# Delta inverse in 32-row corners, and the scaling of the delta rows on VectorE

## What is computed

```python
kb = kc * bc[..., None]
A = jnp.where(strict, einsum("bhncd,bhnsd->bhncs", kb, kc) * decay, 0.0)
rhs = jnp.concatenate([vc * bc[..., None], kb * jnp.exp(gc)[..., None]], axis=-1)
sol = lax.linalg.triangular_solve(A, rhs, left_side=True, lower=True, unit_diagonal=True)
u, w = sol[..., :Dv], sol[..., Dv:]
kdec = kc * jnp.exp(gc[..., -1:] - gc)[..., None]

def step(state, inp):
    v_new = u_i - einsum("bhcd,bhde->bhce", w_i, state)
    o = einsum("bhcd,bhde->bhce", qg_i, state) + einsum("bhcs,bhse->bhce", aqk_i, v_new)
    state = state * gl_i[..., None, None] + einsum("bhcd,bhce->bhde", kdec_i, v_new)
    return state, o
```

## Time and profile before

| | |
|---|---|
| median of three runs | 2746.93 us (2744.68 to 2751.48) |
| the profiled execution | 2750.94 us |
| its span | 2749.2 us, mean granted clock 0.995 |
| TensorE matmul | 2705.3 us busy (98%) |
| TensorE weight load | 2372.3 us (86%) |
| VectorE | 2091.8 us (76%) |
| ScalarE | 1265.3 us (46%) |
| GpSimd | 56.9 us (2%) |
| the delta inverse, first product to `w` | 130.71 to 176.93 us in the first layer |

### The profile page before, as it was taken

How to read it: one execution, slowest core, us unless ns; L and a number is a source line. 1 busy time by engine, 2 the same in 40 slices (tenths; PEclk the granted TensorE clock), 3 DMA queues, 4 the chain that set the end, 5 groups by cost and what they waited for, 6 DMA issues and landing times.

```text
span 2749.2 us, 52010 instructions
## 1 busy us (share of the span) xinstructions
PE 2705.3 (98%) x20739; PEld 2372.3 (86%) x20748; DVE 2091.8 (76%) x3771; ACT 1265.3 (46%) x1926; POOL 56.9 (2%) x89
## 2 busy tenths in 40 slices
PE   9999999999999999999999999999999999999998
PEld 7887898886998689998999998886999999999886
DVE  6766887766775569999666667885999976666787
ACT  4534554433553444455444445442555444444543
POOL 0010000020000000000000000000000000000000
PEclk9999999999999999999999999999999999999999
DMA  5305884314883135643555557663564355555764
GB/s 212 108 34 230 320 325 151 110 41 190 329 329 140 68 129 191 231 150 114 187 193 185 184 192 259 241 232 129 188 230 166 116 177 191 183 185 193 248 243 170
DMA packets 95348, 515.07 MB, mean 187 GB/s; under 512 B 18384, under 2 KB 24912, under 8 KB 38352
## 3 DMA queue, kind: packets, MB, share of 16 engines
q1 hardware_dynamic: 74256, 485.11, 48.9%
q10 hardware_dynamic: 20928, 27.63, 2.9%
HBM read 494.88 MB, written 17.83 MB: 186 GB/s over the span
## 4 chain that ended last, share of the span: by engine, by line
PE 81%; DVE 16%; issue 1%; ACT 1%; DMA 0%; POOL 0%; DVEq 0%; ACTq 0%; SPq 0%; POOLq 0%
PE bank L917 19%; PE bank L905 19%; PE bank L944 12%; PE bank L2089 8%; DVE ring_r L2671 3%; PE bank L2345 3%; PE bank L730 3%; PE bank L581 2%; PE bank L789 2%; PE bank L2363 1%; DVE sb L2754 1%; DVE sb L2745 1%; PE bank L659 1%; DVE sb L2746 1%; PE bank L560 1%
## 5 line engine op out<-in xcount | busy, mean ns | idle before, releaser
L2089 PE MATMUL bank<-peer_pass_high,q_high 128*128 128x256 f32 x1232 | 356.4, 289 | 1.3 <-DVE ring_r L2705 0.8
L2089 PE MATMUL bank<-h_low,q_high 128*128 128x256 f32 x1232 | 347.7, 282 | 0.0
L2089 PE MATMUL bank<-peer_pass_high,ring_r 128*128 128x256 f32 x1232 | 347.1, 282 | 0.0
L917 PE MATMUL bank<-peer_pass_high,peer_pass_hidden 128*128 128x512 f32 x1024 | 339.5, 393 | 0.0
L905 PE MATMUL bank<-peer_pass_high 128*128 128x256 f32 x1008 | 283.2, 281 | 0.0
L905 PE MATMUL bank<-peer_pass_high,ring_r 128*128 128x256 f32 x1008 | 282.9, 281 | 0.0
L905 PE MATMUL bank<-hT_r,peer_pass_high 128*128 128x256 f32 x1008 | 282.9, 281 | 0.0
L1023 DVE TENSOR_TENSOR ring_r<-ring,peer_pass_high 128x1024 fp32r<-128x1024 f32 x128 | 156.8, 1225 | 155.2 <-ACT peer_pass_high L1663 155.2
L2089 PEld LDWEIGHTS bank<-peer_pass_high,q_high 128*128 128x128 f32 x1232 | 233.8, 190 | 1.9 <-DVE ring_r L2705 1.0
L2089 PEld LDWEIGHTS bank<-peer_pass_high,ring_r 128*128 128x128 f32 x1232 | 233.4, 189 | 0.0
L2089 PEld LDWEIGHTS bank<-h_low,q_high 128*128 128x128 f32 x1232 | 232.7, 189 | 0.0
(11 more groups left out here) (431 smaller groups left out, 6324.0 us busy)
## 6 DMA issues: line engine op xcount, KB each, us to landing
ring<-in_experts SPq DMA_DIRECT2D x256, 1024.0 KB, 4.8
ring<-in_w SPq DMA_DIRECT2D x137, 1024.0 KB, 4.8
sb<-in_w_mod SPq DMA_DIRECT2D x48, 1024.0 KB, 6.7
sb<-spill SPq DMA_DIRECT2D x64, 256.0 KB, 5.0
spill<-sb ACTq DMA_DIRECT2D x20, 512.0 KB, 6.5
spill<-sb ACTq DMA_DIRECT2D x48, 128.0 KB, 1.9
sb<-in_ln ACTq DMA_DIRECT2D x8, 512.0 KB, 6.8
sb<-in_post ACTq DMA_DIRECT2D x4, 512.0 KB, 4.6
```

The lines of the kernel that those rows point to most:

```text
L917: m = pe.matmul(ps[4 + 2 * tb + half][:, :], g[:, t], w, start=False, stop=False, skip_group_check=True)
L2089: m = pe.matmul(out, l, r, start=start and i == 0, stop=stop and i == 2)
```

## The change

**Corners of 32.** All stages up to blocks of 32 work on the 32 x 32 corners on the diagonal alone. `products` becomes `corners`: one direction (12 matrices) by four corners, 48 matmuls of 32 x 32 x 32, in one bank, whose 384 columns now hold 12 matrices of 32 columns. The tiles are stored half as wide (names with `_h`), the masks `half_...` too. `LEVELS` has two entries instead of three.

**The last join.** For the step from 32 to 64, TensorE makes `z` (two banks; the corner of A off the diagonal by `TT`), ScalarE copies it out negated, and `inv` (four banks, 36 matmuls each) writes the whole 64 x 64 inverse transposed: the two corners by the identity and the third by `z`. ScalarE copies two of the four banks to `k.TT`, VectorE the other two.

**Scaling.** GpSimd's loop is taken out. VectorE makes `kbg` behind the masks of the levels, `vb` behind level 0, `kdec` behind `inv`, four multiplies each. `kv_scaled` now counts to 12, and TensorE waits for 4 ahead of `w`, 8 ahead of `v`, 12 ahead of the first `kv`.

```diff
-    for g in range(GRP):
-        j += [(("d2", g), "act"), (("d2t", g), "act")]
...
+    for first, second, who in (("d2", "d2t", "act"), ("d4", "p1t", "dve"), ("t", "tt", "act")):
+        for dr in range(2):
+            j += [((first, dr), who), ((second, dr), who)]
...
+    j += [(("z", tb), "act") for tb in range(TB)]
+    j += [(("inv", g), "act" if g % 2 == 0 else "dve") for g in range(GRP)]
...
-LEVELS = ("m8", "m16", "m32")
+LEVELS = ("m8", "m16")
+HALF = 32
...
+    def corner(M, m, q):
+
+        cols = slice(q % 2 * HALF, (q % 2 + 1) * HALF) if M.shape[2] == CHUNK else slice(0, HALF)
+        return M[q * HALF:(q + 1) * HALF, m, cols]
+
+    def corners(key, lhsT, rhs, dr):
 
         b = J.give(pe, key, lay)
-        for h in range(GH):
-            for par in range(2):
-                rows = slice(par * 64, par * 64 + 64)
-                r = rhs[rows, rows] if rhs is c["ident"] else rhs[rows, GH * g + h, :]
-                m = pe.matmul(ps[b][rows, h * 64:h * 64 + 64], lhsT[rows, GH * g + h, :], r, start=True, stop=True)
+        for n in range(TB * GH):
+            for q in range(4):
+                rows = slice(q * HALF, (q + 1) * HALF)
+                r = rhs[rows, rows] if rhs is c["ident"] else corner(rhs, dr * TB * GH + n, q)
+                m = pe.matmul(ps[b][rows, n * HALF:(n + 1) * HALF], corner(lhsT, dr * TB * GH + n, q), r, start=True, stop=True)
         m.then_inc(J.filled, 1)
...
     for lv in range(len(LEVELS)):
...
+        wait(k.LT_ready, lv + 1)
+        for dr in range(2):
+            J.evac(pe, ("t", dr) if lv == 0 else ("ty", lv - 1, dr), lay)
+            corners(("y", lv, dr), k.LT_h[lv], k.T_h, dr)
+        for dr in range(2):
+            J.evac(pe, ("tt", dr) if lv == 0 else ("tyt", lv - 1, dr), lay)
+            J.evac(pe, ("y", lv, dr), lay)
+            corners(("ty", lv, dr), k.TT_h, k.Y_h, dr)
+            corners(("tyt", lv, dr), k.Y_h, k.TT_h, dr)
...
+    J.evac(pe, ("tyt", len(LEVELS) - 1, 1), lay)
+    for tb in range(TB):
+        b = J.give(pe, ("z", tb), lay)
+        for h in range(GH):
+            for dr in range(2):
+                mat = (dr * TB + tb) * GH + h
+                for par in range(2):
+                    far, near = (slice((2 * par + half) * HALF, (2 * par + half + 1) * HALF) for half in (1 - dr, dr))
+                    m = pe.matmul(ps[b][near, h * HALF:(h + 1) * HALF], k.A[far, mat, dr * HALF:(dr + 1) * HALF], k.TT_h[far, mat, :],
+                                  start=True, stop=True)
+        m.then_inc(J.filled, 1)
+    eye = k.cc["eye"]
+    for g, (dr, tb) in enumerate(groups()):
+        J.evac(pe, ("z", tb), lay)
+        b = J.give(pe, ("inv", g), lay)
+        for h in range(GH):
+            mat = g * GH + h
+            for par in range(2):
...
+                pe.matmul(ps[b][far, h * CHUNK:(h + 1) * CHUNK], k.T_h[far, mat, :], eye[far, :], start=True, stop=True)
+                pe.matmul(ps[b][near, own], k.T_h[near, mat, :], eye[near, dr * HALF:(dr + 1) * HALF], start=True, stop=True)
+                m = pe.matmul(ps[b][near, other], k.T_h[near, mat, :], k.Z_h[near, tb * GH + h, :], start=True, stop=True)
+        m.then_inc(J.filled, 1)
+    for g in range(2, GRP):
+        J.evac(pe, ("inv", g), lay)
+    wait(k.kv_scaled, 4)
...
+    def scale_rows(src, dst, f):
+        J.evac(v, ("vn", 1), lay)
+        for dr in range(2):
+            for tb in range(TB):
+                v.tensor_tensor(shaped(dst[:, dr, tb, :], GH, HD), shaped(src[:, tb, :], GH, HD),
+                                bc(f[:, tb, dr * GH:(dr + 1) * GH].unsqueeze(2), GH, HD), ALU.mult).then_inc(k.kv_scaled.sem, 1)
...
+    for lv, (name, i) in enumerate((("half_d8_m8", 1), ("half_m16_eye", 0))):
+        v.tensor_tensor(k.LT_h[lv], k.AT_h, half_mask(name, i, MATS), ALU.mult).then_inc(k.LT_ready.sem, 1)
+    wait(k.beg_ready)
+    scale_rows(k.Kn, k.kbg, k.beg)
...
+        if lv == 0:
+            scale_rows(k.Vn, k.vb, k.beta)
+    for g in range(1, GRP, 2):
+        b = J.take(v, "dve", ("inv", g), lay)
+        v.tensor_copy(part(k.TT, g), shaped(ps[b][:, 0:BLOCKS], GH, CHUNK)).then_inc(J.read["dve"], 1)
+    scale_rows(k.Kn, k.kdec, k.ekd)
...
-    wait(k.beg_ready)
-    J.evac(p, ("vn", 1), lay)
-    for dr in range(2):
-        for tb in range(TB):
-            for src, dst, f in ((k.Kn, k.kbg, k.beg), (k.Kn, k.kdec, k.ekd), (k.Vn, k.vb, k.beta)):
-                m = p.tensor_tensor(shaped(dst[:, dr, tb, :], GH, HD), shaped(src[:, tb, :], GH, HD),
-                                    bc(f[:, tb, dr * GH:(dr + 1) * GH].unsqueeze(2), GH, HD), ALU.mult)
```

More of the change, by code:

```diff
@@ L312, in constants @@
         "d8": (i != j) & (i // 8 == j // 8),
[L313 to L315 removed]
+        "half_d8_m8": np.where(j % CHUNK < HALF, (u != v) & (u // 8 == v // 8), (u // 8 != v // 8) & (u // 16 == v // 16)),
+        "half_m16_eye": np.where(j % CHUNK < HALF, u // 16 != v // 16, u == v),
         "iota": 0 * i + j,
@@ L769, in pe_layer @@
             pe_transpose_heads(k, pe, J, "yd", k.od, lay)
-    J.evac(pe, ("tyt", len(LEVELS) - 1, GRP - 1), lay)
-    wait(k.kv_scaled)
+    J.evac(pe, ("tyt", len(LEVELS) - 1, 1), lay)
+    for tb in range(TB):
+        b = J.give(pe, ("z", tb), lay)
+        for h in range(GH):
+            for dr in range(2):
+                mat = (dr * TB + tb) * GH + h
[11 more added lines that the diff above has]
+            for par in range(2):
+                far, near = (slice((2 * par + half) * HALF, (2 * par + half + 1) * HALF) for half in (1 - dr, dr))
+                own, other = (slice(h * CHUNK + half * HALF, h * CHUNK + (half + 1) * HALF) for half in (dr, 1 - dr))
+                pe.matmul(ps[b][far, h * CHUNK:(h + 1) * CHUNK], k.T_h[far, mat, :], eye[far, :], start=True, stop=True)
[5 more added lines that the diff above has]
+    wait(k.kv_scaled, 4)
     for dr in range(2):
@@ L801, in pe_layer @@
             wait(k.state_zeroed)
+            wait(k.kv_scaled, 8)
         else:
@@ L825, in pe_layer @@
         J.evac(pe, ("v", n), lay)
+        if n == 0:
+            wait(k.kv_scaled)
         if n < 3:
@@ L1357, in dve_layer @@
             v.tensor_tensor(od, od, bc(k.onorm[:, :].unsqueeze(2), 12, HD), ALU.mult).then_inc(k.od_ready.sem, 1)
[L1358 to L1363, removed]
+        for dr in range(2):
+            accumulate(("ty", lv, dr), k.T_h, dr, ALU.subtract)
+            accumulate(("tyt", lv, dr), k.TT_h, dr, ALU.subtract)
+        if lv == 0:
[4 more added lines that the diff above has]
+    scale_rows(k.Kn, k.kdec, k.ekd)
     J.evac(v, "cv", lay)
@@ L1588, in act_layer, with corners @@
     out_head(DH - 1)
[L1589 to L1593, removed]
+    def corners(key, M, dr):
+        copy(key, M[:, dr * TB * GH:(dr + 1) * TB * GH, :], lambda t: shaped(t[:, 0:BLOCKS], TB * GH, HALF))
+    for dr in range(2):
+        corners(("at", dr), k.AT_h, dr)
     for name, dst in (("kn", k.Kn), ("vn", k.Vn)):
@@ L1596, in act_layer @@
             copy((name, tb), dst[:, tb, :], 384)
[L1597 to L1602, removed]
+    for dr in range(2):
+        corners(("d2", dr), k.D2_h, dr)
+        corners(("d2t", dr), k.D2T_h, dr)
+    for dr in range(2):
+        corners(("t", dr), k.T_h, dr)
+        corners(("tt", dr), k.TT_h, dr)
     wait(k.sub_ready)
     for lv in range(len(LEVELS)):
-        for g in range(GRP):
-            stack(("y", lv, g), k.Y, g)
+        for dr in range(2):
+            corners(("y", lv, dr), k.Y_h, dr)
         if lv == 0:
@@ L1612, in act_layer @@
                 a.dma_start(k.post[i], k.dram["post1"][bass.ds(lay, 1), i * D:(i + 1) * D].to_broadcast([P, D])).then_inc(k.post_loaded, 16)
+    for tb in range(TB):
+        copy(("z", tb), k.Z_h[:, tb * GH:(tb + 1) * GH, :], lambda t: shaped(t[:, 0:GH * HALF], GH, HALF), scale=-1.0)
+    for g in range(0, GRP, 2):
+        copy(("inv", g), k.TT[:, GH * g:GH * g + GH, :], lambda t: shaped(t[:, 0:BLOCKS], GH, CHUNK))
     for t in range(3):
```

105 lines of the change are left out of this document (44 added, 61 removed).

## The result

The changed kernel takes 2835.93 us (median of four runs, 2831.24 to 2837.71) where the kernel before takes 2745.80 in the same session: a ratio of 1.032, with an interval of 1.030 to 1.034. It is 3.2% slower. The forecast was 2829, its range 2785 to 2862. The profiled execution took 2837.71 us, its span 2835.9, 86.7 longer than the span before.

The account below looks back on a forecast made before the run. Delivery of TensorE's program in 256-instruction blocks was taken to bound the inverse stage; doubled instructions at 3.8 us a block add 41.7 and 40.5 us, 82 in all: 2746.93 + 82 = 2829, range 2785 to 2862.

Parts of the forecast that it names:

- The block's period: Delta inverse stage: TensorE's program arrives in blocks of 256 instructions, one per 3.8 us, ends 3.5 and 4.25.
- three starved blocks: Blocks of TensorE's program in the kernel before, between holes called "issue", read as 3.96 to 3.97 us each.
- The shift: Output product behind `w` starts 41.7 us later in the first layer, 40.5 in the second: in all 82 us.
- half a block less: Second layer's delta inverse: it begins half a block further on, so its shift was taken as 40.5 us.
- Small pairs in the array: Corner products on four diagonal tiles: 8 ns a load-and-matmul pair, bounds 7.3 and 15, not entering the sum.
- The clock: New stage: 1.2 GHz level stays hidden in blocks; at `w` and the output product up to 3 us a layer.
- The scaling: Twelve row multiplies moved from GpSimd to VectorE: about 0.5 us each, 6 us a layer, hidden; no gain at `w`.
- The first, blocks as fast as they are eaten: Rival for the inverse stage: array sets the pace, `w` 15 us earlier a layer, total 2717; chance 0.10.
- The second, blocks free and 14.5 ns a pair: Rival: 32-column pairs cost as much as 64-column ones, `w` 2 us later a layer, total 2751; chance 0.05.
- The step I trusted least: New inverse stage: delivery stays at its starved pace when blocks are eaten four times as fast.
- The third, the slow end of 4.25: Rival inside the main case: delivery at 4.25 us a block and a low clock behind it, 2852 to 2858.

Follow-up runs that it names:

- the run with the tiny matmuls: Kernel before with 640 bf16 matmuls of zeros, 32 by 32, written out between last `at` and transposes in both layers: 2788.53 us, ratio 1.0146.
- the run with the zero matmuls: Kernel after with a 512-column bf16 matmul of zeros behind every third matrix of each corner group: 2841.19 us, ratio 1.0339 to the kernel before.
- both runs on it: Kernel after with scaling back on GpSimd: 2834.26 us, ratio 1.031; kernel before with scaling on VectorE in the same three places: 2748.89 us, ratio 1.000.
- the same groups from a shorter program: Kernel after with each two neighbouring corner groups replaced by a hardware loop executing the first twice: 2774.51 us, ratio 1.0096 to the kernel before.

## Why the prediction was right

**The block's period.** I took 3.8 us with ends of 3.5 and 4.25, from three starved blocks. The regular bursts of after come 3.72 us apart (3.3 to 4.0 singly). The first product starts at 133.22, 2.5 us later than before, from something ahead of the stage. The other runs of this document, none of them changed ahead of it, begin it anywhere from 128.6 to 134.9, so these 2.5 us need not come from the change. From the block's start at 129.0 + 2.5 to L824 at 223.14 it is 91.6 us for 24.0 blocks, 3.82 each. The difference to 3.72 is in part one long hole, 4.53 us before 196.72 (4.23 in the second layer, 4.53 in the run with the scaling on GpSimd). It comes behind the transposes of the heads. The DMA queues of after, 190 to 194.2 and 194.2 to 196 us, show that the packet itself is late:

```profile
q10 hardware_dynamic: 253, 0.97, 75.8%
```

```profile
q10 hardware_dynamic: 35, 0.08, 11.0%
q8 instruction: 1, 0.02, 3.1%
```

By the count of matmuls a block begins near 190.7. Its packet would be due about 1.1 us later, as in the run with the tiny matmuls, and moves only once the transfers of `in_post` on queue q10 are nearly over, some 3.5 us after the block's start. So the kernel's own transfers are the likely cause of this hole, but no run took them away, and it is not shown.

**The shift.** From the first product to the output product it is 89.9 us instead of 47.8 (178.49 - 130.71) in the first layer, 42.1 more; I had 41.7. In part that is luck: the regular period was 3.72 and not 3.8, and the late packet, which I did not foresee, put about 1.9 us back (196.72 instead of 187.40 + 2 x 3.72), just what 24 blocks at 0.08 less take away. In the second layer I had 40.5, for half a block less. The rows of the second layer:

```profile
597.25 1.66 PE L740 MATMUL bank<-sb 32*32 32x32 f32 x170
...
687.98 2.68 PE L824 MATMUL bank<-ring,sb 128*128 128x512 f32 x4
```

That is 90.7, against 48.5 before (552.76 to 601.28), 42.2 more. The half block made no difference; this term was 1.7 too small. The sum of the profiled execution is 2.5 + 42.1 + 42.2 = 86.8, its span is 86.7 longer, and I had 82. The median rose by 90.1, some 3 us more than the profiled pair shows, within the spread of the runs.

**Small pairs in the array.** I had 8 ns, between 7.3 and 15. The first burst of after, 82 matmuls in 0.90 us, less the last one's 0.2, gives 8.6 at the full clock, and the later ones (1.93 us for 128) 13.6 at 1.2 GHz. As said, it doesn't enter the sum.

**The clock.** The low level came at 143 us, and held for nearly all the rest of the stage. It cost what was left open, 1.2 us at `w` (2.84 against 1.63) and 1.0 at the output product (2.99 against 1.99). The second does not reach the total: at the next layer's first product the lag is 44.5 (597.25 - 552.76), as it was at L824 (223.14 - 178.49 = 44.7). That the clock did nothing else is what the run with the zero matmuls says, and the first blocks of after, at the full clock.

**The scaling.** Nothing, as forecast; both runs on it agree. On VectorE the three sets of four took 1.95 us each in the kernel after, too.

**The rivals.** The first, blocks as fast as they are eaten, would have given 2717, and falls with the 640 tiny matmuls: 3.81 us a block (3.60 in the second layer), though nothing else held TensorE up. The second, blocks free and 14.5 ns a pair, falls with the pace of 8.6 ns and with the same groups from a shorter program. The step I trusted least, that delivery keeps its starved pace when blocks are eaten four times as fast, held: 3.96 then, 3.72 now. They were eaten two to three times as fast, not four: a block was 1.31 to 1.93 us of work instead of 3.7, and 1.2 in the run with the tiny matmuls. The third, the slow end of 4.25, was not met.

## What to carry to other kernels

Where TensorE runs small matmuls, count instructions before array time: an f32 matmul is four of them, a block of 256 took 3.6 to 3.8 us to arrive on average, whatever was in it, so under about 14.5 ns an instruction the program sets the pace and a smaller tile that needs more matmuls makes it slower. The sign in a profile is a run of holes called "issue" at whole multiples of 256 instructions, with a few packets of the instruction queue beside them; in this kernel even one to three such holes of a few tenths a layer said that the stage had no room left. What helps then is fewer instructions for the same work, not a faster array. A hardware loop over a body of many instructions did it here (2774.51 instead of 2835.93); larger tiles would by the same count, of which these runs have only 64 rows against 32.

## What the runs showed of the hardware beyond that

- Ten passes of a loop over 128 instructions took 8.2 us and brought no packet of program in, so they built up no lead. The hole of 1.84 us at 181.34 is no proof of that: it comes 36 us later, behind transfers of `in_post` as the long hole of the kernel after does.
- A product of 64 rows with 64 weight columns took 29 ns on two tiles with 64 moving columns and the same with 32. With 32 weight columns, 32 moving and four tiles it took about 14 at 1.2 GHz (1.94 us for 126, less the last one's 0.24). Which of the two, fewer weights or more tiles, did it is not parted.
- Four tiles on the diagonal, 32 rows each, write one bank at 8.6 ns a matmul. The Trainium skill, page "TensorEngine Tiling (Array Packing)", section "Restrictions and Gotchas", says that different row tiles can't access one PSUM bank at the same time. The kernel after does this without any wait between the tiles, its output is the reference's, and a start every 8.6 ns shows no sign of it; no run writes to four banks instead, so whether that would be faster still is open.
